# Hybrid gated-delta-rule block on one core: chunk inverse doubled from blocks of 2 on 32x32 TensorE tiles, and the first units of the input projection set among the token norms

## What is computed

```python
g = lax.cumsum(chunks(g), axis=3)
decay = jnp.exp(jnp.where(causal, g[..., :, None] - g[..., None, :], -jnp.inf))
kb = k * beta[..., None]
lower = jnp.where(strict, jnp.einsum('bhncd,bhnsd->bhncs', kb, k) * decay, 0.0)
tinv = lax.linalg.triangular_solve(lower + eye, jnp.broadcast_to(eye, lower.shape),
                                   left_side=True, lower=True, unit_diagonal=True)
u = jnp.einsum('bhncs,bhnsv->bhncv', tinv, v * beta[..., None])
w = jnp.einsum('bhncs,bhnsd->bhncd', tinv, kb * jnp.exp(g)[..., None])
...
def hybrid_mixer(u, w_in, ...):
    proj = jnp.einsum('bld,dp->blp', u, w_in)        # u = rms_norm(h, norm_mix)
    qkv, z, b_raw, a_raw, pool_in, gate_pre = jnp.split(proj, offsets, axis=-1)
```

## Time and profile before

| what | value |
|---|---|
| median of 3 runs | 1842.59 us (1842.28 to 1844.46) |
| profiled execution, its own time | 1844.31 us |
| span of the profiled execution | 1842.5 us |
| PE busy in the span | 1753.2 us (95%) |
| DVE, ACT, POOL busy | 951.0, 634.5, 485.8 us |
| first unit on PE starts | 37.52 us |
| chunk loop on PE | about 445 to 938 us |

### The profile page before, as it was taken

One profiled execution on the slowest core, in us unless ns is written; L12 is line 12 of the kernel. 1 busy time (PEld: TensorE's weight loads), 2 busy tenths in 40 slices (PEclk: granted clock), 3 DMA queues, 4 the chain that ended last, 5 costly groups with the idle time before them and its releaser, 6 DMA issues.

```text
span 1842.5 us, 30292 instructions
## 1 busy us (share of the span) xinstructions
PE 1753.2 (95%) x11793; PEld 1680.6 (91%) x11793; DVE 951.0 (52%) x1068; ACT 634.5 (34%) x1026; POOL 485.8 (26%) x468
## 2 busy tenths in 40 slices
PE   5999999986999999999978989999999999999997
PEld 4999999985999999999978989899899999999996
DVE  5344545562556655665553256454564554455457
ACT  6544443344353335333522243112222122122213
POOL 3222222123333434343411113212212122122120
PEclk9999999998999999999989999999999999999999
DMA  6133323224223422342377111111111111111112
GB/s 185 56 90 88 94 84 97 86 81 149 64 74 105 117 63 74 105 117 63 74 239 229 35 35 58 46 34 57 46 34 57 46 34 59 44 46 57 34 46 91
DMA packets 189850, 147.00 MB, mean 80 GB/s; under 512 B 22940, under 2 KB 178115, under 8 KB 188660
## 3 DMA queue, kind: packets, MB, share of 16 engines
q1 hardware_dynamic: 148740, 114.88, 21.4%
q10 hardware_dynamic: 40848, 31.49, 5.5%
q0 software_dynamic: 224, 0.12, 0.0%
HBM read 109.72 MB, written 36.74 MB: 79 GB/s over the span
## 4 chain that ended last, share of the span: by engine, by line
PE 85%; DVE 5%; issue 3%; DMA 2%; ACT 2%; POOL 1%; DVEq 1%; POOLq 1%; SPq 0%; ACTq 0%
PE gb L709 60%; PE db L987 12%; PE db L814 5%; PE db L811 2%; PE db L750 1%; DMA yo<-ot_d 1%; PE db L866 1%; PE db L865 1%; DVE hx L1677 1%; DVE nmx L1539 1%; DVE form L1466 0%; PE db L940 0%; DVE fino L1783 0%; PE db L722 0%; ACT hx L1033 0%
## 5 line engine op out<-in xcount | busy, mean ns | idle before, releaser
L709 PE MATMUL gb<-u_hi,w_hi 128*128 128x342 f32 (+2 forms) x2520 | 824.3, 327 | 18.6 <-ACT ht L1275 7.4
L709 PE MATMUL gb<-u_lo,w_hi 128*128 128x342 f32 (+2 forms) x2520 | 810.5, 322 | 0.0
L709 PE MATMUL gb<-u_hi,w_lo 128*128 128x342 f32 (+2 forms) x2520 | 807.4, 320 | 0.0
L605 POOL TENSOR_TENSOR w_lo<-w_raw,w_hi 128x1024 fp32r<-128x1024 f32 x128 | 338.2, 2648 | 1082.3 <-ACT w_hi L1029 1082.3
L709 PEld LDWEIGHTS gb<-u_hi,w_hi 128*128 128x128 f32 x2520 | 478.3, 190 | 22.1 <-issue 19.3
L709 PEld LDWEIGHTS gb<-u_lo,w_hi 128*128 128x128 f32 x2520 | 478.4, 190 | 0.5
L709 PEld LDWEIGHTS gb<-u_hi,w_lo 128*128 128x128 f32 x2520 | 477.8, 190 | 0.0
L1749 DVE TENSOR_TENSOR h<-h,db 128x512 f32<-128x512 f32 x176 | 117.1, 684 | 59.0 <-PE db L987 58.6
L987 PE MATMUL db<-w_hi,a_hi 128*128 128x512 f32 x352 | 140.7, 400 | 2.9 <-DVE a_lo L1773 2.9
L1029 ACT ACTIVATE w_hi<-w_raw 128x1024 fp32r<-128x1024 f32 x128 | 133.6, 1052 | 18.1 <-ACT tm L1098 13.4
L987 PE MATMUL db<-w_hi,a_lo 128*128 128x512 f32 x352 | 139.7, 397 | 0.0
(11 more groups left out here) (226 smaller groups left out, 1962.6 us busy)
## 6 DMA issues: line engine op xcount, KB each, us to landing
w_raw<-in_w_in SPq DMA_DIRECT2D x53, 512.0 KB, 3.9
w_raw<-in_w_up SPq DMA_DIRECT2D x44, 512.0 KB, 3.8
qkv_d<-tm ACTq DMA_DIRECT2D x24, 576.0 KB, 3.1
tk<-qkv_d SPq DMA_DIRECT2D x9, 1536.0 KB, 8.5
w_raw<-in_w_down SPq DMA_DIRECT2D x22, 512.0 KB, 3.3
ot_d<-ots ACTq DMA_DIRECT2D x9, 512.0 KB, 3.2
yb_d<-ybs ACTq DMA_DIRECT2D x8, 513.0 KB, 3.8
yl<-yb_d SPq DMA_DIRECT2D x8, 513.0 KB, 5.2
```

The source lines that it names most:

```text
L605: pool.tensor_tensor(w_lo[:, n % SLOTS, :], w_raw[:, n % SLOTS, :], w_hi[:, n % SLOTS, :].bitcast(F32), ALU.subtract).then_inc(s_wlo, 1)
L709: mm = pe.matmul(gb[:, bank, 0:w], wt, u, start=(k == 0 and m == 0), stop=(k == KT - 1 and m == 2))
```

## The change

Constants: `LEVELS` goes from [16, 32, 64] to [2, 4, 8, 16, 32, 64], so that the doubling has twelve steps, X0, Y0 to X5, Y5, and no substitution. All intermediate blocks up to 32 lie in four diagonal squares of 32 (`square(p)`): `rrs` holds the four squares of the inverse, side by side for the 8 heads, `tts` the same with each square transposed, `xms` the intermediate product. X0 to X3 and Y0 to Y3 are 32x32 products, four per head, each in rows and columns p of the array; one half bank of `db` takes them all. Behind KK, DVE starts the inverse of blocks of 2 from `at_m`. X4 and Y4 join squares of 32, X5 and Y5 halves of 64; ACT spreads `rrs` and `tts` to `rr` and `tth`. Each tile step has a wait on a constant of `s_const` in addition. POOL's `substitute`, SP's `invert` with its small transfers and the DRAM buffers `blk_d` and `sol_d` are gone. Chunk 0 runs X0 to Y2 in `FIRST_PLAN`.

Start: the constants behind the identity are loaded later, PE turns token tiles 0 to 3 and then takes the first block of tiles W_AB, q 0 and q 1 in half units with one token tile turned between halves, then the blocks 1 and 2 of the three; ACT's `w_high` of them moves in among the tokens, sigmoid and softplus of the beta and g rows move behind tiles 15 to 17, and an early square root on ACT loads its table.

```diff
-LEVELS = [16, 32, 64]
+SMALL = [2, 4, 8, 16]
+LEVELS = SMALL + [32, 64]
+FIRST_LEVELS = 3
...
-FILLS = {"P1": 2, "TKN": 0, "V": 1, "TKB": 0, "GROW": 1, "KK": 2, "TQ": 2, "TKG": 2, "O": 2, "SU": 2, "QK": 1,
-         "TQD": 1, "OT": 5, "X0": 1, "Y0": 2, "X1": 1, "Y1": 1, "X2": 0, "Y2": 1}
+FILLS = {"P1": 2, "TKN": 0, "V": 1, "TKB": 0, "GROW": 1, "KK": 2, "TQ": 1, "TKG": 1, "O": 2, "SU": 1, "QK": 1,
+         "TQD": 1, "OT": 1, "X0": 1, "Y0": 1, "X1": 1, "Y1": 1, "X2": 1, "Y2": 1, "X3": 1, "Y3": 2, "X4": 1,
+         "Y4": 1, "X5": 1, "Y5": 1}
...
 FIRST_PLAN = ["TKN", ("pool", 0), "TKB", ("pool", 1), "GROW", ("pool", 2), ("pool", 3), "KK", ("pool", 4), "TQ",
-              ("pool", 5), ("pool", 6), ("pool", 7), "TKG", "QK", "TQD"]
+              ("pool", 5), ("pool", 6), "X0", ("pool", 7), "Y0", "TKG", "X1", "QK", "Y1", "TQD", "X2", "Y2"]
...
             sp.dma_start(gmix[0:META, :], norm_mix.broadcast_to([META, D])).then_inc(s_gmix, 16)
-            sp.dma_start(cst[:, :], consts).then_inc(s_const, 16)
             sp.dma_start(xt[:, 1, :], x[0, 0:P, :]).then_inc(s_x[1], 16)
             sp.dma_start(gmix[META:, :], norm_mix.broadcast_to([P - META, D])).then_inc(s_gmix, 16)
+            sp.dma_start(cst[:, C_ID:C_ID + P], consts[:, C_ID:C_ID + P]).then_inc(s_const, 16)
...
+                if j in (4, 6):
+                    load_w(W_QKV + j // 2 - 2, cols(w_in, (j // 2 - 2) * P))
+            sp.dma_start(cst[:, P:], consts[:, P:]).then_inc(s_const, 16)
...
-            substitute(0, 1)
             w_low(W_ZG + 2)
...
+            pool.memset(rr[:, :, :], 0.0).then_inc(s_zero, 1)
...
                 mask(i + 1)
-                substitute(i + 1)
...
+            for j in range(FIRST_TOKENS[0] + 1):
+                turn_tokens(j)
+            later = list(range(FIRST_TOKENS[0] + 1, KT + 1))
             for b, (o, w) in enumerate(BLOCKS):
-                unit(W_AB, b, o, w).then_inc(s_g, 1)
...
+                for n in range(3):
+                    q = 3 * b + n
+                    w_ready(W_AB + n)
+                    if q >= 3:
+                        pe.wait_ge(s_gfree, q - 2)
+                    for hf in range(2):
+                        if later:
+                            turn_tokens(later.pop(0))
+                        if n == 0 and hf == 0:
+                            pe.wait_ge(s_u, 2 * (FIRST_TOKENS[b] + 1))
+                        mm = unit(W_AB + n, n, o, w, 4 * hf, 4 * hf + 4)
+                    mm.then_inc(s_g, 1)
...
+                def squares(inputs, op):
+
+                    for h in range(2):
+                        settled()
+                        if freed:
+                            pe.wait_ge(s_ev[freed[0]], freed[1] + h + 1)
+                        for s, v in inputs:
+                            pe.wait_ge(s, v + h + 1)
+                        for m in range(4 * h, 4 * h + 4):
+                            t = op(db[:, bank, m * SQ:(m + 1) * SQ], m)
+                        t.then_inc(s_ps[name], 1)
...
+                elif name in SMALL_X:
+                    settled()
+                    pe.wait_ge(s_tt[int(name[1])], turns(int(name[1]), c))
+
+                    def lower(o, m):
+                        for p in range(P // SQ):
+                            t = pe.matmul(o[square(p), :], at_m[square(p), m, square(p)], tts[square(p), m, :],
+                                          start=True, stop=True)
                         return t
-                    each([(s_tt, 2 * (c - 1))], left_squares)
...
+                    squares([], lower)
...
+                if j in (2, 3, 5):
+                    w_high(W_AB + (2, 3, 5).index(j))
+                elif j == 6:
+                    act.wait_ge(s_hd, 32)
+                    act.wait_ge(s_zero, 3)
+                    ab_taken(0)
...
+                elif name == SMALL_Y[-1]:
+                    act.wait_ge(s_ps["V"], 2 * c)
+                    act.wait_ge(s_tt[len(SMALL)], c)
+                    for p in range(2):
+                        act.activation(tth[square(p), :, square(p)], tts[square(p), :, :], ACT.Copy)
+                    for p in range(P // SQ):
+                        t = act.activation(rr[square(p), :, square(p)], rrs[square(p), :, :], ACT.Copy)
+                    t.then_inc(s_rd, 1)
...
                         dve.tensor_tensor(heads(at_m, h), dbank(name, h), heads(ex, h), ALU.mult).then_inc(s_ev[name], 1)
+                    drain()
+                    if not first(c):
+                        dve.wait_ge(s_rd, c)
+                    for p in range(P // SQ):
+                        dve.tensor_tensor(rrs[square(p), :, :], at_m[square(p), :, square(p)],
+                                          level(len(SMALL))[square(p), :, :], ALU.mult)
+                    drain()
+                    dve.tensor_tensor(rrs[:, :, :], rrs[:, :, :], level(len(SMALL) + 1), ALU.add)
+                    drain()
+                    dve.transpose(tts, rrs[:, :, :]).then_inc(s_tt[0], 1)
                     scaled("qn", 0, 0, FQ, c)
...
+                elif name in SMALL_X:
+                    dve.wait_ge(s_ps[name], 2 * c + (2 if name in EARLY else 0))
+                    dve.tensor_tensor(xms, dsquares(name), level(int(name[1])), ALU.mult).then_inc(s_ev[name], 2)
+                elif name in SMALL_Y:
+                    dve.wait_ge(s_ps[name], 2 * c + (2 if name in EARLY else 0))
+                    dve.tensor_tensor(rrs[:, :, :], rrs[:, :, :], dsquares(name), ALU.subtract).then_inc(s_ev[name], 2)
+                    drain()
+                    dve.transpose(tts, rrs[:, :, :]).then_inc(s_tt[int(name[1]) + 1], 1)
```

More of the change, by code:

```diff
@@ L160, with turns @@
                                 if OBLOCKS[b][0] < _cols)
+FIRST_TOKENS = [-(-(o + w - META) // P) for o, w in BLOCKS]
 NORMED = [-(-(o + w - HALO) // P) + 1 for o, w in OBLOCKS]
+SMALL_X, SMALL_Y = ([f"{s}{n}" for n in range(len(SMALL))] for s in "XY")
+EARLY = [LAST_Y] + SMALL_X[:FIRST_LEVELS] + SMALL_Y[:FIRST_LEVELS]
+def turns(n, c):
+    return c + 1 if n <= FIRST_LEVELS else c
 def pieces_after(name):
@@ L711, in unit, with turn_tokens @@
                 return mm
-            pe.wait_ge(s_const, 16)
-            for j in range(KT + 1):
+            def turn_tokens(j):
                 pe.wait_ge(s_xs, j + 1)
@@ L751, in turn @@
                     t.then_inc(s_tmps, 1)
-            for n in range(3):
-                project(W_QKV + n, U_QKV + 3 * n)
-                if n:
-                    turn(n - 1, n == 1)
+            project(W_QKV + 2, U_QKV + 6, blocks=(0, 1))
+            turn(0, True)
+            project(W_QKV + 2, U_QKV + 6, blocks=(2,))
+            turn(1)
             with pe.Fori(0, QKV_TILES // 3 - 1) as i:
@@ L851, in step @@
-                    each([done["X1"], done["Y0"]], right_squares)
+                        return pe.matmul(o[square(1), :], rrs[square(1), m, :], xms[square(1), m, :],
+                                         start=True, stop=True)
+                    squares([done[SQ_X], done[SMALL_Y[-1]]], right_squares)
                 elif name == TOP_X:
-                    each([done["Y1"]], lambda o, m: pe.matmul(
-                        o[side(m), 0:HALF], at_m[:, m, HALF:], tt_m[:, m, 0:HALF], start=True, stop=True))
+                    settled()
@@ L855, in step @@
+                    pe.wait_ge(s_rd, c + 1)
+                    each([done[SQ_Y]], lambda o, m: pe.matmul(
+                        o[side(m), 0:HALF], at_m[0:HALF, m, HALF:], tth[:, m, :], start=True, stop=True), True)
                 elif name == LAST_Y:
                     each([done[TOP_X]], lambda o, m: pe.matmul(
-                        o[side(m), 0:HALF], nmx[:, m, 0:HALF], rr[:, m, HALF:], start=True, stop=True))
+                        o[side(m), 0:HALF], nmx[HALF:, m, 0:HALF], rr[HALF:, m, HALF:], start=True, stop=True), True)
@@ L878, in _ @@
             pe.wait_ge(s_tm, QKV_TILES)
+            first_steps = [name for name in FIRST_PLAN if isinstance(name, str)]
             for name in FIRST_PLAN:
@@ new lines, in _ @@
+            for b in range(3):
+                if b:
+                    ab_taken(b)
+                if b == 2:
+                    w_high(W_QKV + 2)
+                for n in range(2):
+                    qkv_taken(n, b)
+                    if b == 2:
+                        w_high(W_QKV + 3 + n)
+                if b == 0:
+                    act.wait_ge(s_prmT, 1)
+                    for r, (p0, m) in enumerate(((0, R_CF), (R_CF, 88), (R_CF + 88, 44))):
+                        act.activation(prm[:, p0:p0 + m], mb[:, r * P:r * P + m], ACT.Copy).then_inc(s_prm, 1)
@@ L1121, in qkv_tile @@
                     by_tokens(n - 1, squared)
-            act.wait_ge(s_zero, 3)
-            for j in range(3):
-                qkv_tile(j)
+            for b, (o, w) in enumerate(BLOCKS):
+                act.wait_ge(s_g, U_QKV + 6 + b + 1)
```

(7 more changed lines are left out.)

295 lines of the change are left out of this document (125 added, 170 removed).

## The result

| | before | after |
|---|---|---|
| median of four runs each, us | 1843.53 (1842.28 to 1845.83) | 1955.09 (1950.67 to 1961.06) |
| profiled execution: its own time / span, us | 1844.31 / 1842.5 | 1957.45 / 1955.6 |
| first unit of the fourth pooling tile starts (unit matmul 2017; below, the second stretch of units) | 387.71 | 378.02 |
| P1 of the first chunk | 445.33 | 442.90 |
| one pass of the chunk loop, mean of seven | 61.30 | 75.56 |

The changed kernel is slower: ratio 1.0607, 95% interval 1.0578 to 1.0635. 1875 us with 1850 to 1908 was predicted; the direction was right, the size was not. The spans differ by 113.1 us: the start is 9.7 shorter (378.02 less 387.71), the first chunk 7.3 longer, the eight passes of the loop 112.7 longer (605.3 in place of 492.6), the rest 2.9 longer.

A forecast was written before the change was run, and what follows sets the result against it. PE, busy 95% of the span, was taken as the bound. Terms -7.3 - 3 + 20 + 18 + 4 + 1 = +32.7 on 1844.3 gave 1877.0, 1875 as median; range 1850 to 1908.

The forecast's parts named there:

- term 1: PE's own work per loop pass: 64-instruction small steps at 0.87 us each, +2.5 us a pass, +20 us in eight.
- Rival A: Small steps in the loop: row groups take turns writing one PSUM bank, +29 us, 1905; chance 0.14 with anything above it.
- the prediction's last part: Signs to look for, among them a group of 32x32 matmuls in the loop with 64 starts within about 0.55 us.
- Term 2: DVE between KK and TQ: six new operations delay form `qn`, so TQ waits 2.3 us a pass, +18 us.
- Term 3: Shorter fills further on in a pass: small waits at X2 and Y2, 0.5 us a pass, +4 us.
- Term 4: The start: units among token norms and constants loaded later, nine units ending at 66.3 instead of 74.5, -7.3 us.
- Term 5: The first chunk: without substitution POOL's zeros come earlier, so PE's wait before P1 shrinks, -3 us.
- Term 6: The clock: one half-clock spell behind TQ's new wait in eight passes at least half the time, +1 us.

## Why the prediction was wrong in size

- **The step that failed** is the sum of term 1, and with it the frame of the whole sum: "PE's own work in a pass" priced 512 small instructions a pass (eight steps of 64) by the time they occupy the array, and nothing in the working asked where they come from. No term stood for it. With four heads to an instruction a pass is 8.4 us shorter, 0.9 of which are the small steps' own work; the other 7.5, stops and the half clock behind them, are the missing term, 60 us in eight passes. Before the loop the same edit brings P1 8.2 us forward, the stop of 4.62 us in Y2 among them. A part of the evidence was on the page read for the earlier trace rows, an instruction queue of 25 packets beside an edit that nearly doubles the loop's instructions; that none of them comes in the later passes, one more query would have shown.
- **Term 1's own size** was nearly right: +2.5 us a pass predicted, +2.8 to 2.9 by the rows (+2.0 measured with 16 instructions to a step, and 8 x 0.12 for the step from 16 to 64). 0.87 was taken for a small step and 0.87 to 0.88 measured; Y4 is 0.16 longer than priced. Rival A (row groups taking turns in one bank) did not happen: the 64 starts lie within 0.56 us, as the prediction's last part asked. Gotcha 1 of the Trainium skill ("TensorEngine Tiling (Array Packing)"), which is that rival, and the Trainium skill's floor of about 25 ns between starts ("TensorE: Matmul & The Clock Gate") are both against these rows, in which starts are 9 ns apart.
- **Term 2** was right in place and mechanism and mis-sized by what follows it. The wait was put at 2.3 us and is 2.67 by distance of starts; with the half clock behind it it costs 3.85 a pass, 31 us instead of 18.
- **Term 3** was not there: with TQ's wait and the fetching out, no X or Y step starts more than 0.38 us behind the unit matmul ahead of it, where 0.25 is the change between tile and full-array work. 0.5 us a pass was priced, 0 came.
- **Term 4** was right, -7.3 predicted and -9.7 measured (-9.3 to -10.4 in the profiles of the versions with this start; the bound was -10). The token pace was as assumed; `gmix` came 2.55 us earlier instead of 1.4 and the nine units ended at 62.9 instead of 66.3.
- **Term 5**, with term 4, was forecast as P1 at about 435, and P1 came at 442.90. In the run with four heads to an instruction it is 434.69, but that is luck: the start had given 10.4 (377.29 less 387.71) where 7.3 was priced, and the first chunk behind it 0.2 where 3 was priced. POOL's chain did end early, at 432.2; what P1 then waits for (2.42 us) is DVE's copy of the inverse, behind waits of 3.37 for DVE's form and 2.84 for ACT's kgt. The new steps were forecast to end inside POOL's wait, and they end 2.4 us behind POOL's zeros.
- **Term 6** was mis-sized: one spell of half clock in eight passes at least half the time was forecast; of the 16 in seven passes four lie behind TQ, six behind the stops at P1 and six behind those in or near X1. Their cost is inside the 7.5 and 3.85 above.
- With the missing term taken out by experiment (four heads to an instruction, span 1879.1, 36.6 more than before) the sum of +32.7 is 4 us off: start and first chunk together -10.6 (434.69 less 445.33) where -10.3 was written, the loop +45.7 (538.3 us from first to last P1 in place of 492.6) where terms 1, 2, 3 and 6 had 43, and 1.6 more behind the loop. That it comes so near is in part luck, since errors cancel: 4 less for term 1 (with 16 instructions to a step; with 64 it would be 3 more), 13 more for term 2 with its clock, 4 less for term 3.
- That the range missed has the same cause. Its upper end came from the prices of rival A, another way for PE's instructions to take long, and from no case in which a resource that the rows never showed at its limit becomes one.

The best of all versions is the kernel before with the new start, 1833.5 us. The inverse on PE, even with both disturbances out, puts 2.0 us a pass (2.8 to 2.9 for the right product) on the engine that bounds the loop, to spare POOL work that was hidden.

## What to carry to other kernels

Before a loop's body grows, count its instructions on the engine that bounds it, loads included, and look in the trace for packets of the instruction queue inside the loop: none behind the first pass means that the body stays, and here the first size that didn't stay cost at once at every jump and around many short instructions. A stop in the middle of a group, between two instructions without a semaphore, that ends a nearly fixed time behind a packet's start is the mark of it. An experiment that makes instructions fewer can also make the work itself cheaper: take that part out by the distance of starts before the rest is called fetching. And a wait on a chain at full clock should be priced with the half clock that may follow, which here added half as much again.

## What the runs showed of the hardware that was not expected

- A loop body on PE of 752 matmuls with their loads (1579 recorded instructions) stays with the engine, and one of 816 (1707) is fetched again in every pass, in packets of 16 KB, 8.7 to 9.9 a pass.
- A late packet stops PE for 0.8 to 6.0 us, and PE goes on 2.2 to 2.9 us behind the packet's start, 2.5 to 4.3 us at the jump back. Beside the jumps such stops of over 0.7 us fell inside a run of 32x32 matmuls or within five unit matmuls behind one, and once in Y4; the full-array stream of 1056 matmuls to a body was stopped at the jump alone.
- Four row groups and four column groups run side by side into one PSUM bank: 64 instructions of 32x32 in 0.56 us from first to last start. Half as many instructions of twice the columns shorten a step by 0.11 us (0.88 to 0.77), and half as many again by 0.01.
- A stop of some 2.5 us brings the granted clock to 0.50 for 3.4 us often, but not always: with TQ's wait and no stop beside it in the pass, five of seven passes had it.
